# One decoder step on one core: a table of load orders, state copies from unit 12, pages loaded a stage ahead, sample attention joined with a unit's weights as the held operand

## What is computed

```python
m = silu(c) @ ada_w + ada_b                  # shift, scale, gate, twice: 6 x 1024
h = rmsnorm(x, g) * (1 + scale) + shift
qa, ka, va, qb, kb, vb = split(h @ w_in)     # q and k with rotary
# prompt: causal attention of 1024 tokens in two head groups (differential; dilated)
# sample: the same against paged K/V (kv_pages) and a window state (kv_state)
#         a unit is one sequence and one head group
# differential group: softmax(s1) @ v - lam * softmax(s2) @ v
k_win_sample = concat(state_k_win, kb)[:, 4:]    # v_win_sample alike: 2044 rows copied on
x = x + gate * (concat(oa, ob) @ w_o)        # then a product-key expert layer
```

## Time and profile before

| | us |
|---|---|
| median of 3 runs | 4199.21 |
| lowest and highest | 4194.9 and 4211.27 |
| profiled execution | 4200.97 |
| its span in the trace | 4199.4 |

### The profile page before, as it was taken

How to read it: one execution, slowest core, us unless ns; L and a number is a source line. 1 busy time by engine, 2 the same in 40 slices (tenths; PEclk the granted TensorE clock), 3 DMA queues, 4 the chain that set the end, 5 groups by cost and what they waited for, 6 DMA issues and landing times. The chain is left out here.

```text
span 4199.4 us, 59061 instructions
## 1 busy us (share of the span) xinstructions
PE 3399.6 (81%) x20585; PEld 2924.5 (70%) x20585; DVE 2807.4 (67%) x5853; ACT 1338.2 (32%) x3148; POOL 1690.8 (40%) x1333
## 2 busy tenths in 40 slices
PE   6799688466777688266659999999999999999995
PEld 3578455111544578255559999999999999998994
DVE  3114576001133129999969999889889989998885
ACT  3010466000011111386843333233333333333331
POOL 1011000000000443287865665565556555655650
PEclk8899799767679799676779999999999999999997
DMA  6765543999311233154578988888898889888883
GB/s 238 252 236 206 171 157 127 365 395 407 154 36 56 95 98 106 37 131 98 116 209 314 327 319 314 311 322 316 307 325 319 324 319 328 319 315 298 323 302 150
DMA packets 393741, 1001.85 MB, mean 239 GB/s; under 512 B 186980, under 2 KB 238031, under 8 KB 329752
## 3 DMA queue, kind: packets, MB, share of 16 engines
q1 hardware_dynamic: 327960, 491.18, 34.4%
q0 software_dynamic: 62656, 469.86, 30.9%
q10 hardware_dynamic: 2944, 38.77, 2.5%
HBM read 914.75 MB, written 152.04 MB: 254 GB/s over the span
## 5 line engine op out<-in xcount | busy, mean ns | idle before, releaser
L2014 DVE CUSTOM_DVE_ANT_0 e_uv<-e_uv,e_h 128x1024 f32<-128x1024 f32 x416 | 725.4, 1744 | 78.0 <-DMA e_uv<-peer_uv,k_g_idx 77.3
L2083 POOL DMA_INDIRECT e_uv<-peer_uv,k_g_idx x416 | 522.2, 1255 | 548.5 <-DVE e_pY L2026 507.3
L1321 PE MATMUL e_po<-e_ph,e_vh 128*128 128x320 f32 x2048 | 648.0, 316 | 64.5 <-DVE k_OT L2058 58.4
L1321 PE MATMUL e_pa<-k_hi_d,e_uh 128*128 128x320 f32 x2048 | 639.8, 312 | 50.3 <-POOL e_ul L2074 37.6
L1322 PE MATMUL e_pa<-k_lo_d,e_uh 128*128 128x320 f32 x2048 | 634.4, 310 | 0.0
L1323 PE MATMUL e_pa<-k_hi_d,e_ul 128*128 128x320 f32 x2048 | 634.3, 310 | 0.0
L1322 PE MATMUL e_po<-e_pl,e_vh 128*128 128x320 f32 x2048 | 633.4, 309 | 0.0
L1323 PE MATMUL e_po<-e_ph,e_vl 128*128 128x320 f32 x2048 | 633.4, 309 | 0.0
L2026 DVE SCALAR_TENSOR_TENSOR e_pY<-e_uv,e_wts,e_pY 128x1024 f32<-128x1024 f32 x412 | 525.7, 1276 | 0.0
L1321 PEld LDWEIGHTS e_po<-e_ph,e_vh 128*128 128x128 f32 x2048 | 384.9, 188 | 92.3 <-DVE k_OT L2058 75.9
L1321 PEld LDWEIGHTS e_pa<-k_hi_d,e_uh 128*128 128x128 f32 x2048 | 386.1, 189 | 62.1 <-issue 46.2
(11 more groups left out here) (284 smaller groups left out, 5863.9 us busy)
## 6 DMA issues: line engine op xcount, KB each, us to landing
s_kv<-kv_pages SPq DMA_DIRECT2D x128, 512.0 KB, 6.9
s_kv<-kv_state SPq DMA_DIRECT2D x32, 2048.0 KB, 17.3
e_v<-peer_uv SPq DMA_DIRECT2D x128, 512.0 KB, 6.3
e_u<-peer_ut SPq DMA_DIRECT2D x126, 512.0 KB, 6.2
s_g<-r_G SPq DMA_DIRECT2D x10, 4096.0 KB, 21.0
k_OT<-s_g SPq DMA_DIRECT2D x128, 320.0 KB, 5.5
k_win_sample<-state_k_win ACTq DMA_DIRECT2D x28, 1168.0 KB
v_win_sample<-state_v_win POOLq DMA_DIRECT2D x28, 1168.0 KB, 9.5
```

Of the source, the lines that this page charges most:

```text
L1321: nc.tensor.matmul(out, lhs_hi, rhs_hi, start=start, stop=False)
L2014: nc.vector.tensor_tensor_reduce(uv[:, r, 0:D], uv[:, r, 0:D], h[:], 1.0, 0.0, ALU.mult, ALU.add, dots[:, r:r + 1]).then_inc(row_dotted, 1)
L2083: nc.gpsimd.indirect_dma_start(uv[:, s % RING], None, io["peer_uv"], bass.IndirectOffsetOnAxis(ap=keep.g_idx[:, s:s + 1], axis=0),).then_i ...
```

## The change

In `project` one list gives the order of loads: chunks 0 to 7, halves 0 and 1, chunks 8 to 15, halves 2 and 3, chunks 16 to 20, halves 4 and 5, chunks 21 to 23, halves 6 to 11. `ADA_AT` says after which unit each chunk is multiplied, `SPLIT_AT` at which unit each half is split, `TURN_AT` when a modulation row is turned; `issue_at` is worked out from them: a load is issued at the unit after the one in which its slot was used last. The copies start with unit 12 instead of 6 (`COPIES_AT`), 28 over 38 units. ScalarE splits the first two halves behind the square root and ahead of the row copy, no longer between the squares. A unit waits for each half of its weights where it uses it. The rotary table is loaded at unit 6.

The page table is loaded in `prompt_attn`, and the 16 pages of sequence 0 are loaded there too, behind the last v load; their buffer lives over both stages. The first state load of `sample_attn` waits for nothing.

The join holds a unit's selector weights (128 x 32) and moves its result (512 columns): 16 products into four banks, four units beside each other in the partitions. ScalarE copies each bank to SBUF, TensorE turns it in four pieces, and VectorE takes what belongs to each head from the turned rows.

```diff
-    ADA_AT = {1: 2, 2: 13}
     RING = 8
-    COPIES_AT = 6
+    COPIES_AT = 12
+
+    ADA_AT = {8: 0, 9: 1, 10: 1, 11: 2, 12: 2, 13: 3, 14: 4, 15: 4,
+              16: 8, 17: 9, 18: 10, 19: 11, 20: 12, 21: 14, 22: 17, 23: 18}
+    SPLIT_AT = {2: 5, 3: 6, 4: 13, 5: 14, 6: 20, 7: 21, 8: 30, 9: 31, 10: 39, 11: 40}
+    TURN_AT = {1: 5, 2: 19}
...
+        loads = (chunks(0, 8) + halves(0, 1) + chunks(8, 16) + halves(2, 3) + chunks(16, 21) + halves(4, 5)
+                 + chunks(21, 24) + halves(*range(6, 12)))
         place = {what: n for n, what in enumerate(loads)}
+
+        def used_at(n):
+
+            kind, m = loads[n]
+            return ADA_AT.get(m, -1) if kind == "ada" else SPLIT_AT.get(m, -2) + 1
+
+        issue_at = list(itertools.accumulate([used_at(n - RAW) + 1 if n >= RAW else -1 for n in range(len(loads))], max))
...
-            return min(WIN_SHARES, max(0, n + 1 - COPIES_AT) * WIN_SHARES // (UNITS - 2 * COPIES_AT))
+            return min(WIN_SHARES, max(0, n + 1 - COPIES_AT) * WIN_SHARES // (UNITS - COPIES_AT - 4))
...
+                for n in range(len(loads)):
+                    if issue_at[n] < 0:
+                        load(n)
+                for unit in range(UNITS):
+                    for n in range(len(loads)):
+                        if issue_at[n] == unit:
+                            load(n)
+                    if unit == 6:
+                        sp.wait_ge(late_lo, 1)
...
+                    store(unit)
...
-                    if k in (5, 7):
-                        split_w(k // 6)
                 act.wait_ge(mean_done, 1)
                 nc.scalar.activation(rstd[:], rstd[:], ACT.Sqrt).then_inc(root_done, 1)
+                for m in range(2):
+                    split_w(m)
                 row(0)
...
-                for m in range(2, 4):
-                    split_w(m)
                 for n in range(UNITS):
...
-                    if i == 0:
-                        pe.wait_ge(wlo_done, 2 * gi + 2)
...
+                        if i == 0 and k % HALF == 0:
+                            pe.wait_ge(wlo_done, 2 * gi + k // HALF + 1)
...
+def load_pages(sp, io, keep, b):
+
+    for p in range(PAGES):
+        page = sp.value_load(keep.pages[0:1, b * PAGES + p:b * PAGES + p + 1], min_val=0,
+                             max_val=io["kv_pages"].shape[0] - 1)
+        sp.dma_start(keep.kv0[:, p], io["kv_pages"][ds(page, 1)].rearrange("a p n -> (a p) n")).then_inc(keep.kv0_in, 16)
...
                     sp.dma_start(vv[:, u], view[:, :, 3 * g + 2, cols]).then_inc(v_in[u], 16)
+                sp.wait_ge(pages_in, 16)
+                load_pages(sp, io, keep, 0)
...
-                sp.wait_ge(small_in, 64)
 
                 for b in range(NSEQ):
                     if b:
                         sp.wait_ge(mixed, 2 * b - 1)
...
-                    if b:
+                        load_pages(sp, io, keep, b)
                         sp.wait_ge(mixed, 2 * b)
...
+                for j in range(4):
+                    for n in range(4):
+                        mm = nc.tensor.matmul(pJ[R * n:R * n + R, j], selw[:, 4 * j + n], O[4 * j + n], start=True, stop=True,
+                                              skip_group_check=True)
+                    mm.then_inc(joined, 1)
+                for j in range(4):
+                    pe.wait_ge(joined_out, j + 1)
+                    for c in range(CH):
+                        tr = nc.tensor.transpose(pR[:, j, c * P:(c + 1) * P], J[:, j, c * P:(c + 1) * P], keep.ident[:])
+                tr.then_inc(rows_turned, 1)
...
+                v.wait_ge(rows_turned, 1)
+                got = pR[:].rearrange("p j (c b g r) -> p j c b g r", c=CH, b=2, g=2)
+                for c in range(CH):
+                    first, last = ((2 * c + s) * SQ for s in range(2))
+                    late = keep.OT[:, c, TP:T].rearrange("p (j b q) -> p j b q", j=4, b=2)
+                    nc.vector.tensor_copy(late, got[:, :, c, :, 0, first:first + SQ]).then_inc(first_done, 1)
+                    v.wait_ge(first_done, c + 1)
+                    nc.vector.tensor_tensor(late, late, got[:, :, c, :, 0, last:last + SQ], ALU.add)
+                    for s in range(2):
+                        rows = slice(HD * s, HD * s + HD)
+                        at = (2 * c + s) * SQ
+                        nc.vector.tensor_copy(keep.OT[rows, CH + c, TP:T].rearrange("p (j b q) -> p j b q", j=4, b=2),
+                                              got[rows, :, c, :, 1, at:at + SQ])
...
+                for j in range(4):
+                    act.wait_ge(joined, j + 1)
+                    nc.scalar.activation(J[:, j], pJ[:, j], ACT.Copy).then_inc(joined_out, 1)
```

More of the change, by code:

```diff
@@ L300, in _, with load @@
                 sp.dma_start(keep.halves[:], io["t_halves"]).then_inc(small_in, 16)
+                def load(n):
+                    kind, m = loads[n]
+                    if kind == "ada":
+                        load_ada(m)
+                    else:
+                        load_w(m)
                 for k in range(KC):
                     sp.dma_start(xT[:, k], io["x_t"][:, k]).then_inc(x_in[k], 16)
-                for m in range(2):
-                    load_w(m)
-                for m in range(KC):
-                    load_ada(m)
@@ L897, in sample_attn @@
         new_out = nc.alloc_semaphore("s_new_out")
[L898 removed]
+        kv_in = [keep.kv0_in, nc.alloc_semaphore("s_kv1_in")]
         vnew_in = nc.alloc_semaphore("s_vnew_in")
@@ L2284, in build @@
         keep.OT = sb("k_OT", [P, KC, T])
-        for stage in (project, prompt_attn, sample_attn):
-            run_stage(nc, io, keep, stage)
+        keep.kv0_in = nc.alloc_semaphore("k_kv0_in")
+        run_stage(nc, io, keep, project)
+        with nc.sbuf_tensor("k_pages", [1, NSEQ * PAGES], I32) as keep.pages, \
+                nc.sbuf_tensor("k_kv0", [P, PAGES, 2 * GROUP], F32) as keep.kv0:
+            for stage in (prompt_attn, sample_attn):
+                run_stage(nc, io, keep, stage)
         room = keep.OT[:].rearrange("p k t -> p (k t)")
```

121 lines of the change are left out of this document (43 added, 78 removed).

## The result

The changed kernel took 4149.56 us (median of four runs, 4138.23 to 4167.89). The kernel before took 4197.06 us on the same chip (four runs, 4192.78 to 4211.27). The ratio is 0.9885, with a 95% interval of 0.9838 to 0.9933: some 48 us faster. The forecast was 80 us faster, 4119, with a range up to 4148. A second set of six runs on another chip gave 4141.60 against 4181.36, ratio 0.9903 (0.9885 to 0.9922). The sign was right and the size was not.

A forecast was written before the change was run, and what follows sets the result against it. Projection was taken as bound by TensorE when fed, sample attention by DMA, its end by TensorE. Gains of 24 (projection), 25 (prefetch, at cost 0) and 31 (join) made 80: 4199.2 - 80 = 4119 us, range 4102 to 4148.

The forecast's parts named there:

- Part 4: Projection, 28 copies in 38 units beside the stores: stores fall behind but are covered; 3 us charged, bounds 0 and 25.
- Part 3: Projection, modulation chunk loads from unit 8 on: they go while no copy runs, so 29.4 us of waits go.
- The throttle: Projection: ScalarE must wait for w_in halves 10 and 11, queued with the stores, before issuing the last nine copies.
- The cover: Projection: a store has 12 units, or 67 us, to land before its late landing costs time.
- Part 3's weak chunk: Projection, chunk 21: loaded at about 161, used at 170, beside three copies; 3 us charged, between 0 and 17.
- rival 1: Projection: stores starve in part after unit 26, 20 to 25 us of stall; total 4140, chance 0.22.
- Rival 3: Projection: copies hold stores back wholly, 96 us of stall, 66 lost in projection; total 4209, chance 0.02.
- Part 1: Start of projection: new load order brings the modulation row copy to about 50.9, 2.3 us earlier, bounds 0 and 3.5.
- Parts 2 and 3: Projection's chunk loads: units 0 to 9 lose 10 us as before; from unit 8 on 29.4 us of waits go.
- Part 5: First pages loaded in prompt attention at cost 0, at most 2; sample attention gains 25 us, between 20 and 27.
- rival 2: Copies also slow the page loads in prompt attention: prefetch gives 15, prompt attention ends 3 later; 4132, chance 0.10.
- Part 6: Sample attention's join: 16 products replace 96, 11.7 us against 42.4; 31 us gained, between 28 and 34.

The follow-up runs named there:

- the second profile: The changed kernel run once more, nothing altered, on another chip: 4141.60 us, ratio 0.9903 against the kernel before.
- the run at the pace of before: The changed kernel with its copies started at unit 6 and spread over 42 units, as in the kernel before: 4151.81 us, ratio 0.9916.

## Why the prediction missed

**The step that failed is Part 4, the copies beside the stores.** It charged 3 us over the kernel before, with a bound of 25. From unit 27 to unit 53 before takes 144.65 us, as long as the kernel without copies, and after takes 180.11: the stores cost 35.5 us (29.8 in the second profile). The other 10.3 of the 46 us that the copies cost in all are a chunk's, of Part 3. Three things were wrong in Part 4.

The rate. I took 24 packets a us for SyncE's queue beside the copies, from one window of 22 us in before. That window was a mean over two kinds of time, and its own lines tell them apart. From 334 to 338 us of before, and then from 338 to 346:

```profile
q10 hardware_dynamic: 27, 0.78, 48.5%
q1 hardware_dynamic: 28, 0.06, 3.7%
...
q10 hardware_dynamic: 38, 1.12, 45.2%
q1 hardware_dynamic: 374, 0.72, 40.5%
```

In the first the two queues are even at 7 packets a us, as in after; why SyncE's passes more in the second no run shows. I gave the case in which the copies hold the stores back wholly a chance of 0.02 because "in the fullest stretch of before 24 packets a us did pass". A mean rate of a window was taken for a rate under load. The rule of the Trainium skill that the forecast named against itself (DMA: Bandwidth & Descriptors, section Queues, rings and completion order) is the one that these rows bear out.

The throttle. I argued that ScalarE would hold its last nine copies back, as it waits for weight loads in the queue that is starved. It did wait (31 us at 295), but seven copies had been issued since 238 us, four of them within 2.9 us, and beside them SyncE's queue passed 6 packets a us from 254 to 284 us. At the end of the wait it issued five more at once:

```profile
260.35 2.10 ACTq L615 DMA_DIRECT2D k_win_sample<-state_k_win  x3
...
262.57 0.68 ACTq L615 DMA_DIRECT2D k_win_sample<-state_k_win  x1
...
295.46 1.92 ACT L357 ACTIVATE p_whi<-p_raw 128x2048 fp32r<-128x2048 f32 x1 [30.99 <-DMA p_raw<-w_in]
295.46 3.65 ACTq L615 DMA_DIRECT2D k_win_sample<-state_k_win  x5
```

Before had such bursts too (six copies at 312.53), but from 302 to 312 us, ahead of that burst, no packet of ScalarE's queue moved, and SyncE's passed 186 a us; the stores issued ahead of the burst had landed by 316.3.

The cover. I counted 12 units between a store and the engine that needs its buffer. That counts the landing of a store from its issue, and SyncE itself was held for 40.29 us in an issue, and the stores behind it were not even issued; the cover has to take in both. The kernel before showed such issues in small (8.70 us at 342.90), and the forecast has no term for them. The landings themselves, 57.6, 30.1 and 49.5 us, were under the 67 of cover; TensorE had to wait because the second and third of these stores were issued more than 40 us after their units were done. The three waits of VectorE add up to 54.8 us, and TensorE stood for 11.45 and 18.91 of them, and the granted clock from 297 to 345 us was 0.68, part of it at the lower level of 1.2 GHz.

Against the kernel without K copies, unit 27 was rotated 10.3 us late (265.97 and 255.70) and unit 53, the last, 45.7. The first part is Part 3's weak chunk, of which the forecast said 3, between 0 and 17. TensorE's wait for it, in after:

```profile
203.86 1.90 PE L415 MATMUL p_pM<-p_raw,p_cT 128*9 128x512 f32 x8 [9.44 <-DMA p_raw<-ada_w]
```

It is chunk 22 and not 21, and its stall is 11.6 us by the steps (194.52 to 265.97 is 71.45, without copies 59.84), inside the bounds.

Of the rivals, rival 1 (stores starve in part, projection 3 us shorter, 4140) is the nearest. Its mechanism is the one seen, and its size was too small: it had 20 to 25 us of stall, where the stores cost 30 to 35, and the projection was not 3 us shorter but 22 longer. Rival 3 (held back wholly, 66 longer) overstated: it took the copies as one run of 163 us, and in after their queue ran empty at 294 to 298 us and the stores caught up. The measured case lies between the two. That 4149.56 misses the range by only 1.6 us says little for the sum: the projection missed its forecast by 46 us in the trace, and the spread of the expert stage, which the change leaves alone, gave back 13 to 20 by luck. The sum's own range was also too narrow as written: the low ends of its terms, 0, 20 and 28, make 4151 and not 4133.

**Part 1** forecast the row copy at 50.9; it was at 52.20. The first product was not 2.3 us earlier but 3 later, by the hold of VectorE. No row of before showed such a hold, since there the pass came earlier; the bound of "0 to 3.5" excluded a loss without a reason. **Parts 2 and 3** are right in sum up to unit 17: it was rotated at 194.52 for 217.41, 22.9 us sooner though the first product was 3 us late, so 26 gained where the forecast had 28 ahead of the weak chunk. Part 3's reason, that these chunk loads go while no copy runs, is the one that the run at the pace of before bears out. **Part 5**: 20 to 22 us of sample attention for a forecast of 25, in the range of 20 to 27. In the profile of after GpSimd's last copy is what ends prompt attention (it was issued at 754.97, VectorE had ended at about 762.9, and the next stage began at 768.30), which was rival 2's sign, at a cost of some 4 us; in the second profile the stage took 315.5 and no such cost is seen. **Part 6**: 10.6 us for a forecast of 11.7, gain 31.8 for 31.

Sum with measured terms, against the profile of before: projection -22, prompt attention 0 to -6, prefetch 22, join 32: between 26 and 32 us, and 13 to 20 more from the expert stage's spread in the profiles; the medians say 40 and 48.

## What to carry to other kernels

In this kernel large memory-to-memory copies in one queue were free beside small stores in another as long as their queue ran empty between copies: keep at most one in flight, or put them into a stage in which no engine asks for a transfer as soon as it lands. Beside loads that an engine waits for, even one in flight cost time, 22 us at the chunks and 4 us a copy at the routing weights. A mean rate of a window is no rate under load: ask for the worst few microseconds and count packets of both queues. When a change has several parts, run each alone: here one of three lost 22 us and the sum hid it.

## What was not expected of the hardware

Two queues that both have work are served one packet each, 39 and 39, 33 and 34, 40 and 39, 37 and 38 in four stretches of 6 us, though their packets are of 37 KB and 2 KB, and the engines are busy for about half of that time. An engine that issues a transfer into a queue that isn't drained stands still in the issue itself, 40.29 us for one that usually takes 0.32; the longest issue of a first store was 12.4 us with two copies in flight and 1.0 with one. Two copies in flight cost as much as any number (450.2 and 444.9 us for the stage's end), and one costs nothing at the stores (144.65 us from unit 27 to 53, as without copies). A copy pattern with its rows named apart (2 KB each) still moved in packets of 30 KB in the mean. A VectorE operation of 0.20 us took 4.16, and one of 0.75 took 4.71, when GpSimd's pass of about 4.5 us over the weights was under way. A DMA share of 0.32 was no room: each copy put there cost 4 us, while 16 to 18 copies in a stage with a share of 0.17, in which GpSimd's first low half came 209 us after the start, cost nothing.
